# Gate and up products of a feed-forward in float32r: one matmul of 512 columns for two of 256

## The reference

```python
def swiglu(x, w_gu, w_down):
    g, u = jnp.split(x @ w_gu, 2, axis=-1)
    return (jax.nn.silu(g) * u) @ w_down

u = modulate(rmsnorm(h, norm1_g[l]), mod[:, 0, 0], mod[:, 0, 1])
h = h + FFN_RES_WEIGHT * mod[:, 0, 2][:, None, :] * swiglu(u, ffn1_w_gu[l], ffn1_w_down[l])
```

## Time and profile before

| | us |
|---|---|
| median of 3 runs | 1566.36 |
| lowest and highest | 1563.52, 1570.63 |
| span of the profiled execution | 1493.2 |
| PE busy | 1221.3 |
| DVE busy | 1039.1 |
| ACT busy | 425.9 |

### The profile page before, as it was taken

The page is one execution under the profiler, slowest core; times in us unless marked ns, Lnnn a source line. Parts: engine busy times, 40 slices in busy tenths (PEclk is TensorE's granted clock), DMA queues, the critical chain, the costliest instruction groups (busy, mean ns, idle before and its releaser), DMA issues.

```text
span 1493.2 us, 17594 instructions
## 1 busy us (share of the span) xinstructions
PE 1221.3 (82%) x6525; PEld 888.2 (59%) x6525; DVE 1039.1 (70%) x1903; ACT 425.9 (29%) x740; POOL 582.6 (39%) x644
## 2 busy tenths in 40 slices
PE   6997997677786565665566579999999999999997
PEld 3545675344443222222222229989989999899996
DVE  5786468888688775866666546677777759575655
ACT  1147213021112111211110114333345556243342
POOL 4140026777777777777777742001010000000000
PEclk9999898788998778777788899999999999999999
DMA  9917149999999999999999986888757545357651
GB/s 328 358 42 254 57 171 340 394 409 400 409 409 408 408 400 401 410 408 410 409 410 409 410 350 214 284 286 283 262 182 242 189 165 184 113 170 228 203 187 71
DMA packets 179708, 435.45 MB, mean 292 GB/s; under 512 B 13881, under 2 KB 84610, under 8 KB 179638
## 3 DMA queue, kind: packets, MB, share of 16 engines
q0 software_dynamic: 84384, 306.26, 52.3%
q1 hardware_dynamic: 94214, 126.18, 25.3%
q10 hardware_dynamic: 1040, 2.10, 0.4%
HBM read 433.44 MB, written 2.14 MB: 292 GB/s over the span
## 4 chain that ended last, share of the span: by engine, by line
PE 47%; POOL 28%; issue 10%; DVE 6%; DMA 5%; ACT 2%; SPq 0%; DVEq 0%; POOLq 0%
POOL arena L795 21%; PE quad L1505 14%; POOL ring L795 7%; PE quad_a L1610 7%; PE quad_a L1519 6%; PE quad_a L1204 4%; DMA ring<-in_ffn_w_gu_dram 3%; PE quad_a L1459 2%; PE quad_a L1305 2%; PE quad L1287 2%; DMA arena<-in_peer_v_dram,arena 2%; PE quad_a L1687 2%; PE quad_a L1675 2%; PE quad_a L1533 1%; ACT arena L823 1%
## 5 line engine op out<-in xcount | busy, mean ns | idle before, releaser
L1459 PE MATMUL quad_a<-arena 128*128 128x512 f32 x384 | 200.0, 685 | 124.0 <-DMA arena<-in_peer_v_dram,arena 124.0
L1459 PEld LDWEIGHTS quad_a<-arena 128*128 128x128 f32 x384 | 84.5, 225 | 238.9 <-issue 238.6
L795 POOL DMA_INDIRECT arena<-in_peer_v_dram,arena x193 | 186.0, 964 | 61.8 <-issue 58.0
L1505 PE MATMUL quad<-u_hi,w_hi 128*128 128x256 f32 x704 | 199.5, 283 | 0.6 <-DVE u_lo L2018 0.6
L1505 PE MATMUL quad<-u_lo,w_hi 128*128 128x256 f32 x704 | 199.2, 283 | 0.0
L1505 PE MATMUL quad<-u_hi,w_lo 128*128 128x256 f32 x704 | 199.0, 283 | 0.0
L795 POOL DMA_INDIRECT arena<-in_peer_u_dram,arena x168 | 170.9, 1017 | 58.7 <-issue 50.6
L722 POOL DMA_DIRECT2D arena<-in_w_ada_dram x60 | 31.8, 531 | 401.0 <-DVE arena L1753 398.8
L1976 DVE TENSOR_TENSOR w_lo<-ring,w_hi 128x2048 fp32r<-128x2048 f32 x66 | 150.7, 2289 | 52.2 <-ACT w_hi L994 52.0
L988 ACT ACTIVATE arena<-ident,arena 128x128 f32<-128x128 f32 x192 | 59.6, 389 | 343.4 <-DVE arena L2123 343.4
L2133 DVE SCALAR_TENSOR_TENSOR hx<-arena,hx 128x1024 f32<-128x1024 f32 x46 | 59.1, 1284 | 135.9 <-DMA arena<-in_peer_v_dram,arena 135.6
(11 more groups left out here) (374 smaller groups left out, 2415.0 us busy)
## 6 DMA issues: line engine op xcount, KB each, us to landing
ring<-in_ffn_w_gu_dram SPq DMA_DIRECT2D x44, 1024.0 KB, 9.1
arena<-in_w_ada_dram POOLq DMA_DIRECT2D x60, 512.0 KB, 6.3
ring<-in_ffn_w_down_dram SPq DMA_DIRECT2D x22, 1024.0 KB, 5.0
ring<-in_w_mix_in_dram SPq DMA_DIRECT2D x20, 1024.0 KB, 6.6
arena<-in_peer_w_query_dram SPq DMA_DIRECT2D x4, 2048.0 KB, 9.8
ring<-in_w_ada_dram POOLq DMA_DIRECT2D x12, 512.0 KB, 10.4
arena<-in_w_in_dram SPq DMA_DIRECT2D x3, 2048.0 KB, 35.7
arena<-in_w_out_dram SPq DMA_DIRECT2D x2, 2048.0 KB, 11.3
```

The costliest lines, as they stand in the source:

```text
L795: gp.indirect_dma_start(out=rows_of(n), out_offset=None, in_=t["peer_" + kind][0], in_offset=bass.IndirectOffsetOnAxis(ap=expert[tt][:, sl ...
L1459: last = te.matmul(sum_side[tt][:, cols], diag[:, i % DIAGS], rows_of(n)[:, cols], start=(slot == pe_slots[0]), stop=(slot == pe_slots[-1] ...
L1505: last = te.matmul(psum[c][:, w * SEQ:(w + 1) * SEQ], weight[a][:, k, (c % 2) * P:(c % 2 + 1) * P], (u_hi, u_lo)[b][:, k], start=(k == 0 a ...
```

## The change

The low and the high part of u now lie in one tensor, and a matmul with the high weights takes both as its 512 columns; its result has two halves, high weights by low u and high weights by high u. A second matmul of 256 columns adds the low weights by high u to the second half. Gate and up of a tile have a bank each, so a tile takes two banks and two tiles fit in `quad` instead of four. ScalarE copies the first halves of both banks to SBUF (`pair_sum`), VectorE adds the second halves, and Silu and the product by up read `pair_sum`. up(j) waits for the pair sum of tile j-2. In VectorE's order the pair sum comes first, then the `w_ada` sums, then Silu's consumer. The wait for h of tile 19 goes, and in the second feed-forward `modulation(2, 0, 1)` moves behind the first group of last down products.

```diff
+        u_parted = rounded("u_parted", arena_at, 0, 2 * KD * SEQ)
+        u_lo, u_hi = (u_parted[:, KD * SEQ * i:KD * SEQ * (i + 1)].rearrange("p (k n) -> p k n", k=KD) for i in range(2))
+        u_both = u_parted.rearrange("p (w k n) -> p k w n", w=2, k=KD)
+        pair_sum = area(arena, 23048, 4 * SEQ).rearrange("p (b w n) -> p b w n", b=2, w=2)
+        pairs_at = [quad[:, 1024 * i:1024 * (i + 1)].rearrange("p (w x n) -> p w x n", w=2, x=2) for i in range(2)]
...
@@ silu_part
-                    ac.activation(silu[:, c % 2], psum[c][:, 0:SEQ], ACT.Silu).then_inc(silu_ready.sem, 1)
+                    ac.activation(pair_sum[:, c % 2], pairs_at[c % 2][:, :, 0], ACT.Copy).then_inc(low_out.sem, 1)
+                    sc_e.wait_ge(pair_summed.sem, j + (f * FT + 1))
+                    ac.activation(silu[:, c % 2], pair_sum[:, c % 2, 0], ACT.Silu).then_inc(silu_ready.sem, 1)
...
@@ up
-                    if f or not isinstance(j, int) or j >= 4:
-                        pe.wait_ge(h_ready.sem, j + (f * FT - 3))
+                    if f or not isinstance(j, int) or j >= 2:
+                        pe.wait_ge(pair_summed.sem, j + (f * FT - 1))
...
-                            for n, (a, b) in enumerate(THREE):
-                                last = te.matmul(psum[c][:, w * SEQ:(w + 1) * SEQ], weight[a][:, k, (c % 2) * P:(c % 2 + 1) * P], (u_hi, u_lo)[b][:, k],
-                                                 start=(k == 0 and n == 0), stop=(k == KD - 1 and n == 2), skip_group_check=True)
+                            cols, both = slice((c % 2) * P, (c % 2 + 1) * P), pairs_at[c % 2][:, w]
+                            te.matmul(both, weight[0][:, k, cols], u_both[:, k], start=(k == 0), stop=False, skip_group_check=True)
+                            last = te.matmul(both[:, 1], weight[1][:, k, cols], u_hi[:, k], start=False, stop=(k == KD - 1), skip_group_check=True)
...
@@ end of ffn
-                pe.wait_ge(h_ready.sem, f * FT + 20)
-                if f:
-                    modulation(2, 0, 1)
                 for n in range(2):
                     last_downs(0, n)
+                    if f and n == 0:
+                        modulation(2, 0, 1)
...
@@ ffn_rows
+                def pair(j, c):
+                    ve.wait_ge(low_out.sem, j + (f * FT + 1))
+                    v.tensor_tensor(pair_sum[:, c % 2], pairs_at[c % 2][:, :, 1], pair_sum[:, c % 2], ALU.add).then_inc(pair_summed.sem, 1)
+
...
-                    v.tensor_tensor(hT[:, c], silu[:, c % 2], psum[c][:, SEQ:], ALU.mult).then_inc(h_order.sem, 1)
+                    v.tensor_tensor(hT[:, c], silu[:, c % 2], pair_sum[:, c % 2, 1], ALU.mult).then_inc(h_order.sem, 1)
...
                 def tile_and_sums(j, c):
-                    tile(j, c)
+                    pair(j, c)
                     if f == 0 and j >= 2:
                         sum_ada(2 if j % 5 in (0, 2, 4) else 1)
                     elif f and 2 <= j < 18 and j % 2 == 0:
                         sum_ada(1)
+                    tile(j, c)
```

More of the change, by code:

```diff
@@ L326, in program @@
         merged_lo = rounded("merged_lo", arena_at, 15880, KD * SEQ).rearrange("p (k n) -> p k n", k=KD)
-        u_lo = rounded("u_lo", arena_at, 0, KD * SEQ).rearrange("p (k n) -> p k n", k=KD)
-        u_hi = rounded("u_hi", arena_at, 2048, KD * SEQ).rearrange("p (k n) -> p k n", k=KD)
+        u_parted = rounded("u_parted", arena_at, 0, 2 * KD * SEQ)
+        u_lo, u_hi = (u_parted[:, KD * SEQ * i:KD * SEQ * (i + 1)].rearrange("p (k n) -> p k n", k=KD) for i in range(2))
+        u_both = u_parted.rearrange("p (w k n) -> p k w n", w=2, k=KD)
         h_lo = rounded("h_lo", arena_at, 4608, 4 * SEQ).rearrange("p (b n) -> p b n", b=4)
         h_hi = rounded("h_hi", arena_at, 5632, 4 * SEQ).rearrange("p (b n) -> p b n", b=4)
+        pair_sum = area(arena, 23048, 4 * SEQ).rearrange("p (b w n) -> p b w n", b=2, w=2)
         later = sb("later", P)[:]
@@ L393, in program @@
         rdiag = [gain_rows, lam_in.rearrange("p v d -> p (v d)")[:, 0:P]]
+        low_out, pair_summed = signal("low_out"), signal("pair_summed")
         u_hi_ready, u_split, h_order = signal("u_hi_ready"), signal("u_split"), signal("h_order")
```

## The result

| | before | after |
|---|---|---|
| median, us (6 runs each, one chip) | 1565.36 | 1575.54 |
| lowest and highest | 1563.52, 1570.63 | 1571.55, 1580.30 |
| profiled execution's span | 1493.2 | 1570.8 |

The ratio is 1.0068, with a 95% interval from 1.0050 to 1.0086: slower by 10.2 us, and by more than can be taken for no change. Forecast were 1567.4 us and "within 0.5%".

What follows compares the result with a forecast made beforehand. TensorE was taken as the bound in both feed-forwards. -7.6 + 4.2 + 2.0 + 1.2 + 1.2 = +1.0 us gave span 1494.2 and time 1567.4 us; the forecast's own range was 1564 to 1571, with rivals 1560 to 1575.

Steps and rivals of the forecast that it cites:

- TensorE, -7.6 forecast: Both feed-forwards: two 256-column matmuls (0.2400 us) become one of 512 (0.2292), 0.0108 us less, 704 times: 7.6 us saved.
- The rival of no gain: Merged matmuls, both feed-forwards: 512 columns from two stretches still cost 0.240 us, costs of 8.6 stand alone, 1575 us; 5%.
- First feed-forward, middle, +4.2 forecast: Down products waiting for their weights' low half: each block 1.24 us nearer a stall, stalls 7.8 us instead of 3.6.
- the rival of later landings: First feed-forward: one more w_ada row ahead of the second gate/up load, 1.3 us later per block; 1572.2 us; 16%.
- the 15 us that the prediction named as a sign of being wrong: Weight loads: landings more than 15 us after a block's start would show the forecast wrong.
- The rival of stalls that don't grow: First feed-forward, middle: a stall gives transfers time, so landings could move earlier with it; -3.2 us, 1563.2 us; 17%.
- the clock drop: Either feed-forward: a granted clock below 1.00 inside the stage would show the forecast wrong; no size given.
- First feed-forward, end, +2.0 forecast: VectorE's chain into the next stage, taken as later than TensorE's wait for h, starts 5.05 us after tile 21, before 3.0.
- Second feed-forward, start, +1.2 forecast: Tile 2's weights' low half, behind copy, table load and Silu, is ready at 6.8 us, due at 5.6: 1.2 us.
- this hand-over: Second feed-forward, middle: added add and handing over of the Silu make down weights ready by 20.8 us against 22.26; hidden.
- Second feed-forward, end, +1.2 forecast: Last down products: nine matmuls take 2.06 us, tile 21's h comes at 3.3, so TensorE waits 1.2 us.
- The 73.2 us outside the span: Whole kernel: median 1566.36 us less span 1493.2 us, taken to lie outside the span and carried over unchanged.

## Why the prediction was wrong

It had the sign and much of the mechanism. Its sum lacked 9.1 of the 10.1 us that the stages show. Three of its steps failed: the price that it gave the merged matmuls, the path that it took for the later one at the end of the first feed-forward, and a wait at the start of the second that it left out. Step by step:

- **TensorE, -7.6 forecast, -3.6 measured.** The price of 256 columns was read at the last two tiles alone (0.1200), where the middle of the stage pays 0.119; and that of 512 at the down products (0.229), where between 256s it is 0.233. Two small errors on both sides of a small difference: 0.08 us a tile in 40 tiles, 0.115 in four. The rival of no gain is wrong too (5.1 ns a merger, not 0), but it lay nearer. The Trainium skill (TensorE: Matmul & The Clock Gate, "Back-to-back issue gap") gives a warm matmul a fixed part of about 2.5 ns, so that as an estimate a merger saves as much; the trace has 5.1, twice that and half of the 10.8 that the prediction set against it.
- **First feed-forward, middle, +4.2 forecast, +5.3 measured.** The mechanism stands: a chain of 10.7 us, stalls at the forecast place in six blocks, none left there when the order is turned. Stalls are 8.9 us where 7.8 were forecast, although TensorE, at 5.63 us a tile, was due 0.1 us later than thought. Landings in blocks 2 to 8 came 0.5 us later in the mean (from a block's first up product to ScalarE's rounding of the second load 14.23 us, before 13.72), and that is nearly all in blocks 5 and 8: 16.43 and 15.45 us, before 14.24 and 14.61. So the rival of later landings holds in two blocks of seven, past the 15 us that the prediction named as a sign of being wrong, but not for its reason: GpSimd issued as many pieces of `w_ada` between the block's start and these two landings as before (four and three). What made them late stays open. The rival of stalls that don't grow is out. To this comes the clock drop, 1.7 us, which the prediction had named only as a sign of being wrong, at no price. The stage's middle grew by 5.5 us net: 5.3 of stalls and 1.7 of clock, less 1.6 of shorter tiles, which are counted with TensorE.
- **First feed-forward, end, +2.0 forecast, +2.7 measured, and for another reason.** The step that failed is "the chain over VectorE is the later one". PE, DVE and ACT in order of time, first before, then after (compare):

```profile
1087.51 3.63 PE L1412 MATMUL quad<-ones,arena 128*128 128x1 f32 x32
...
1094.37 0.16 DVE L1998 RECIPROCAL rstd<-rstd 128x1 f32<-128x1 f32 x1 [2.68 <-ACT rstd L1000]
```

```profile
1154.45 0.39 PE L1539 MATMUL quad_a<-w_hi,h_hi 128*128 128x512 f32 x1
...
1159.13 0.50 PE L1539 MATMUL quad_a<-w_hi,h_hi 128*128 128x512 f32 x1 [1.90 <-DVE h_lo L2218]
1162.70 3.63 PE L1418 MATMUL quad<-ones,arena 128*128 128x1 f32 x32
...
1165.62 0.16 DVE L1998 TENSOR_TENSOR stats<-stats 128x1 f32<-128x1 f32 x1
1169.57 0.16 DVE L2003 RECIPROCAL rstd<-rstd 128x1 f32<-128x1 f32 x1 [3.79 <-ACT rstd L1004]
...
1167.33 0.60 ACT L1069 ACTIVATE arena<-quad 128x512 f32<-128x512 f32 x1 [0.78 <-PE quad L1420]
...
1169.24 0.29 ACT L1004 ACTIVATE rstd<-stats,eps 128x1 f32<-128x1 f32 x1
```

  VectorE's sums are ready at 1165.78, and then it waits 3.79 us for ScalarE's root. ScalarE's queue has the modulation's copy ahead of that root, and this one waits for TensorE's modulation matmuls (L1418), which start 8.25 us after tile 21 where it was 5.56: 2.69 us later, by its 2.2 us of waits above all. VectorE waits for the root in the trace of before as well, 2.68 us; the prediction followed one branch through and not the one that ended last. The run with h ahead of the sums bears it out: VectorE's chain started 1.1 us later and the stage's end stayed.
- **Second feed-forward, start, +1.2 forecast, +2.6 measured.** The wait at tile 2 is there with 1.10 us. Missed, at no price in the sum, are the 1.53 us at the first down product. ACT, DVE and PE in order of time:

```profile
1378.54 1.28 ACT L1057 ACT_TABLE_LOAD   x1
...
1387.23 0.42 ACT L1057 ACTIVATE arena<-arena 128x256 f32<-128x256 f32 x1 [2.88 <-DVE arena L2207]
1387.55 1.90 ACT L998 ACTIVATE w_hi<-ring 128x2048 fp32r<-128x2048 f32 x1
...
1382.10 4.49 DVE L1981 TENSOR_TENSOR w_lo<-ring,w_hi 128x2048 fp32r<-128x2048 f32 x2 [0.59 <-ACT w_hi L998]
1386.51 0.68 DVE L2207 TENSOR_TENSOR arena<-quad,arena 128x512 f32<-128x512 f32 x1
...
1389.49 2.29 DVE L1981 TENSOR_TENSOR w_lo<-ring,w_hi 128x2048 fp32r<-128x2048 f32 x1 [0.59 <-ACT w_hi L998]
...
1391.93 0.70 PE L1525 MATMUL quad_a<-w_hi,h_hi 128*128 128x512 f32 x2 [1.53 <-DVE w_lo L1981]
```

  Tile 1's copy is there at 1384.35, but its sum is queued on VectorE behind two low halves, and the Silu behind the sum (2.88 us), and the down weights' rounding behind the Silu. The prediction named this hand-over for the middle of the stage, where the loads come late enough, and did not price it at the start, where the weights are all there and VectorE has no idle time.
- **Second feed-forward, end, +1.2 forecast, +1.4 measured.** The wait for h is 1.01 us, the last part is 22.37 us against 20.99 with the modulation in it.
- **The 73.2 us outside the span** were no such thing. They didn't touch the sum, since both times were taken with them.

With the measured terms (-3.6, +5.3 and +1.7 of clock, +2.7, +2.6, +1.4) the sum is +10.1. Of the 9.1 us to the forecast's +1.0, TensorE's pitch is 4.0, the middle of the first stage with its clock 2.8, the second's start 1.4 and the two ends 0.9. The clock drop, 1.7 us of it, is the least certain: the kernel before, run once more, had one too.

## What to carry to other kernels

A merged instruction saves only the difference between two pitches, so read both in the neighbourhood in which the new one will stand, and over many tiles; here 0.17 us a tile became 0.08, in 44 tiles, against two added hand-overs. Where an engine's queue gets a step that waits for another engine (copy, sum, Silu), price it at the start and the end of a stage, where nothing is late that could hide it, and follow every branch to the instruction that was released last. The stalls themselves were an order on two queues: what is needed first (the down weights) stood behind what came last, and turning that was worth some 12 us to the changed kernel (from 10.2 behind before on one chip to 2.3 ahead on another) and 5 to the old one.

## What the runs showed of the hardware

The same program takes 1495.79, 1563.65, 1565.46 or 1572.6 us on different chips. Nearly all of the 68 to 77 us between the first and the others lies ahead of the first feed-forward, which begins at 899.6 to 902.6 us in the traces of the one kind and at 967.1 to 982.4 in those of the other, in the stage that fetches rows (394 against 360 GB/s).

A stall can cost more than its length. Of sixteen stalls of 2.1 us or more in the first feed-forward's middle, over eight traces, ten were followed by a down tile of 4.05 to 4.46 us with a mean clock of 0.62 to 0.68 (so most of it at the 1.2 GHz level), and six were not; after the shorter stalls there the clock stayed at 1.00. Such a tile takes 1.2 to 1.7 us more than one at full clock. It isn't a bound: behind a wait of 1.9 us in the last down products the clock fell in the changed kernel with the order turned and stayed at 1.00 in after. What decides was not tested.

Silu of 128x256 takes 0.42 us from SBUF, where it took 0.38 from PSUM; the copy of 128x512 takes 0.60 and the sum 0.68, as forecast.
